# Two feed-forward networks on one core: other weight slots for the second up-chunk and the last down-chunk

## The reference

```
# first block: D_FF = 2816, depthwise conv of width 3 over the tokens
h2 = modulate(rms_norm(x, g_norm2), shift2, scale2)
u = causal_depthwise_conv(h2 @ w_up, w_conv, b_conv)
val, gte = split(u, 2)
x = x + (1 + gate2) * ((val * silu(gte)) @ w_down)
# second block: D_FF_2 = 4096
f = square(relu(x @ w_up + b_up)) @ w_down + b_down
x = layer_norm(ALPHA * x + f, ln3_g, ln3_b)
```

## Time and profile before

| what | value |
|---|---|
| time, median of 3 runs | 3761.49 us (3753.72 to 3762.09) |
| profiled execution, time | 3759.51 us |
| its span | 3757.8 us |
| PE busy | 3127.0 us (83%) |
| DVE, ACT, POOL busy | 1794.4, 955.4, 963.9 us |
| first network, first to last matmul | 933.62 to about 1703.7 us |
| second network, first to last matmul | 2995.02 to about 3715.0 us |

### The profile page before, as it was taken

The page is one execution under the profiler, slowest core; times in us unless marked ns, Lnnn a source line. Parts: engine busy times, 40 slices in busy tenths (PEclk is TensorE's granted clock), DMA queues, the critical chain, the costliest instruction groups (busy, mean ns, idle before and its releaser), DMA issues. The chain is left out here.

```text
span 3757.8 us, 42220 instructions
## 1 busy us (share of the span) xinstructions
PE 3127.0 (83%) x16524; PEld 2674.7 (71%) x16524; DVE 1794.4 (48%) x2896; ACT 955.4 (25%) x1387; POOL 963.9 (26%) x336
## 2 busy tenths in 40 slices
PE   8687999676899999974858637978888699999994
PEld 6576999475688888863746636778668678888883
DVE  1411767335355555456168956872233433333334
ACT  0101544221222122212056534641222211111111
POOL 0312332112223232223012422211301233333333
PEclk9798999587999999986978868999899799999997
DMA  7462232221101111101122322131132111111101
GB/s 265 103 109 83 67 84 51 101 93 48 45 34 56 45 56 45 45 11 51 59 71 76 113 65 69 49 106 34 45 135 103 44 45 45 45 45 66 46 34 56
DMA packets 111989, 257.33 MB, mean 68 GB/s; under 512 B 49761, under 2 KB 71732, under 8 KB 95591
## 3 DMA queue, kind: packets, MB, share of 16 engines
q1 hardware_dynamic: 110439, 252.24, 20.0%
q0 software_dynamic: 1408, 3.15, 1.5%
HBM read 208.33 MB, written 47.03 MB: 68 GB/s over the span
## 5 line engine op out<-in xcount | busy, mean ns | idle before, releaser
L836 PE MATMUL psum<-h_hi,w_hl 128*128 128x512 f32 x2432 | 756.6, 393 | 27.2 <-POOL w_hl L825 23.2
L825 POOL TENSOR_TENSOR w_hl<-w_raw,w_hl 128x2048 fp32r<-128x2048 f32 x65 | 323.5, 4979 | 1012.8 <-ACT w_hl L819 1012.8
L849 PE MATMUL psum<-w_hl,ffn_a_hi 128*128 128x512 f32 x1728 | 540.0, 394 | 30.3 <-issue 30.3
L836 PEld LDWEIGHTS psum<-h_hi,w_hl 128*128 128x128 f32 x2432 | 460.7, 190 | 125.7 <-POOL w_hl L825 24.4
L836 PE MATMUL psum<-h_lo,w_hl 128*128 128x512 f32 x1216 | 476.8, 392 | 0.0
L610 PE MATMUL psum<-w_hl,h_hi 128*128 128x256 f32 (+1 forms) x2048 | 380.9, 289 | 32.0 <-POOL w_hl L571 14.7
L849 PEld LDWEIGHTS psum<-w_hl,ffn_a_hi 128*128 128x128 f32 x1728 | 326.8, 189 | 102.8 <-issue 31.1
L610 PE MATMUL psum<-h_hi,w_hl 128*128 128x512 f32 (+1 forms) x1152 | 349.7, 388 | 53.1 <-POOL w_hl L571 27.3
L610 PEld LDWEIGHTS psum<-w_hl,h_hi 128*128 128x128 f32 x2048 | 329.3, 198 | 34.1 <-issue 18.7
L571 POOL TENSOR_TENSOR w_hl<-w_raw,w_hl 128x2048 fp32r<-128x2048 f32 (+1 forms) x39 | 177.6, 4555 | 680.3 <-ACT w_hl L563 667.2
L849 PE MATMUL psum<-w_hl,ffn_a_lo 128*128 128x512 f32 x864 | 340.1, 394 | 0.0
(11 more groups left out here) (286 smaller groups left out, 5018.3 us busy)
## 6 DMA issues: line engine op xcount, KB each, us to landing
w_raw<-in_w_up SPq DMA_DIRECT2D x38, 1024.0 KB, 4.8
w_raw<-in_w_down SPq DMA_DIRECT2D x27, 1024.0 KB, 4.8
ada_w<-in_w_ada SPq DMA_DIRECT2D x24, 1024.0 KB, 4.7
w_raw<-in_w_in_T SPq DMA_DIRECT2D x12, 1024.0 KB, 6.9
t_y<-mix SPq DMA_DIRECT2D x24, 512.0 KB, 4.8
w_raw<-in_xa_wkv SPq DMA_DIRECT2D x8, 1024.0 KB, 5.7
w_raw<-in_w_in_G SPq DMA_DIRECT2D x8, 648.0 KB, 5.3
p1G<-sb_stage SPq DMA_DIRECT2D x16, 324.0 KB, 3.7
```

Source lines behind the costliest of these rows:

```text
L825: pool.tensor_tensor(self.k.w_lo[s][:, :], self.k.w_raw[s][:, :], self.k.w_hi[s][:, :].bitcast(F), ALU.subtract).then_inc(self.k.wsem["w_r ...
L836: m = pe.matmul(k.bank[b][:, :], w[:, t * CW + f * P:t * CW + (f + 1) * P], h[:, t, half * 512:half * 512 + 512], start=t == 0 and w is k. ...
L849: m = pe.matmul(k.bank[4 + out % 4][:, :], a[:, f, tile * P:(tile + 1) * P], w[:, f * D + half * 512:f * D + half * 512 + 512], start=f == ...
```

## The change

It changes the two networks alone, and computes the same. In both, the second up-chunk is loaded early into slot 1 instead of the first down-chunk. In the first network slot 0 holds up(0), up(2), up(3) and so on to up(21), and at its end the last down-chunk; slot 1 holds up(1) and then down-chunks 0 to 9. In the second network slot 0 holds up(0) and then down-chunks 0 to 14, slot 1 holds up(1) to up(15) and at its end down(15). The activations for the last down-chunk are written to buffers of their own (`last_hi`, `last_lo`). At the end of the first network PE does 5 outputs of down(9) before up(21) and 11 behind it, and DVE's order there is add 0 to 4, convolution of chunk 20, product, gating of the last down-chunk, convolution of chunk 21, add 5 to 8, product of chunk 21, add 9 to 15. The core of the diff:

```
-        ... self.first = k, uses, (w_up[0, :, :], w_down[0, :, :])
+        ... self.first = k, uses, (w_up[0, :, :], w_up[1, :, :])
...
 # ffn_conv, sync
-                wt.load(sp, 0, 1, w_up[1, :, :])
-                wt.load(sp, 1, 0, w_down[0, :, :])
+                wt.load(sp, 1, 0, w_up[1, :, :])
                 def body(j):
-                    g = j + 1
-                    wt.load(sp, 0, 2 * g, w_up[2 * g, :, :])
-                    wt.load(sp, 0, 2 * g + 1, w_up[2 * g + 1, :, :])
-                    wt.load(sp, 1, g, w_down[g, :, :])
+                    wt.load(sp, 0, 2 * j + 1, w_up[2 * j + 2, :, :])
+                    wt.load(sp, 1, j + 1, w_down[j, :, :])
+                    wt.load(sp, 0, 2 * j + 2, w_up[2 * j + 3, :, :])
                 looped(sp, G - 1, body)
+                wt.load(sp, 0, NF1 - 1, w_down[G - 1, :, :])
...
 # ffn_conv, tensor
-                looped(pe, G - 2, body)
-                down(G - 1, range(16))
+                looped(pe, G - 3, body)
+                up(NF1 - 2)
+                down(G - 2, range(5))
+                up(NF1 - 1)
+                down(G - 2, range(5, 16))
+                pe.wait_ge(*wt.at("w_ready", 0, NF1))
+                pe.wait_ge(a_lo_done, NF1)
+                for o in range(16):
+                    down_products(k, pe, last_hi, last_lo, o, dn_mm,
+                                  lambda: pe.wait_ge(dn_out, 16 * (G - 1) + o - 3), 0)
...
 # ffn_conv, scalar, start
-                w_up_hi(0)
-                evac_first(0, 0)
-                w_up_hi(1)
+                wt.split_hi(act, 0, 0)
+                wt.split_hi(act, 1, 0)
+                evac_first(0, 0)
+                w_up_hi(2)
                 silu(0, 0)
                 evac_first(1, 1)
-                w_up_hi(2)
+                act.wait_ge(up_mm, 8)
                 w_down_hi(0)
...
 # ffn_conv, scalar, end
+                a_part(2 * g, 0, last_hi)
                 evac(2 * g + 1, 1)
-                w_down_hi(g)
-                a_part(2 * g, 0)
+                act.wait_ge(up_mm, 4 * NF1)
+                act.wait_ge(w_gated, 2 * G)
+                wt.split_hi(act, 0, NF1 - 1)
                 silu(2 * g + 1, 1)
-                a_part(2 * g + 1, 1)
+                a_part(2 * g + 1, 1, last_hi)
...
 # ffn_conv, vector, end
-                looped(dve, G - 1, body)
+                looped(dve, G - 2, body)
+                add_down(G - 2, range(5))
+                conv_steps(NF1 - 2, 0, False)
+                times_silu(NF1 - 2, 0)
+                gate_w_down(G - 1, 0, NF1 - 1)
+                conv_steps(NF1 - 1, 1, False)
+                add_down(G - 2, range(5, 9))
+                times_silu(NF1 - 1, 1)
+                add_down(G - 2, range(9, 16))
                 add_down(G - 1, range(16))
...
 # ffn_squared_relu, sync
+                wt.load(sp, 0, 0, w_up[0, :, :])
                 def body(g):
-                    wt.load(sp, 0, g, w_up[g, :, :])
-                    wt.load(sp, 1, g, w_down[g, :, :])
-                looped(sp, G, body)
+                    wt.load(sp, 1, g, w_up[g + 1, :, :])
+                    wt.load(sp, 0, g + 1, w_down[g, :, :])
+                looped(sp, G - 1, body)
+                wt.load(sp, 1, G - 1, w_down[G - 1, :, :])
...
 # ffn_squared_relu, scalar
+                act.wait_ge(up_mm, 4 * G)
+                wt.split_hi(act, 1, G - 1)
+                act.wait_ge(squared, G)
+                act.activation(last_hi[:, :, :], r[:, :, :], ACT.Copy).then_inc(a_hi_done, 1)
```

More of the change, by code:

```diff
@@ L785, in __init__ @@
     def __init__(self, k, uses, w_up, w_down):
-        self.k, self.uses, self.first = k, uses, (w_up[0, :, :], w_down[0, :, :])
+        self.k, self.uses, self.first = k, uses, (w_up[0, :, :], w_up[1, :, :])
         self.early_done = {"load": 0, "hi": 0, "lo": 0}
@@ L826, in split_lo, with up_products @@
                                ALU.subtract).then_inc(self.k.wsem["w_ready"][s], 1)
-def up_products(k, pe, hh, hl, mm):
+def up_products(k, pe, hh, hl, mm, slot=0):
+    w_hi, w_lo = k.w_hi[slot], k.w_lo[slot]
     for f in range(2):
@@ L834, in up_products, with down_products @@
             for t in range(KT):
-                for w, h in ((k.w_hi[0], hh), (k.w_lo[0], hh), (k.w_hi[0], hl)):
+                for w, h in ((w_hi, hh), (w_lo, hh), (w_hi, hl)):
                     m = pe.matmul(k.bank[b][:, :], w[:, t * CW + f * P:t * CW + (f + 1) * P],
                                   h[:, t, half * 512:half * 512 + 512],
-                                  start=t == 0 and w is k.w_hi[0] and h is hh,
+                                  start=t == 0 and w is w_hi and h is hh,
                                   stop=t == KT - 1 and h is hl)
             m.then_inc(mm, 1)
-def down_products(k, pe, a_hi, a_lo, out, mm, waits):
+def down_products(k, pe, a_hi, a_lo, out, mm, waits, slot=1):
     tile, half = out // 2, out % 2
@@ L847, in down_products @@
     for f in range(2):
-        for n, (w, a) in enumerate(((k.w_hi[1], a_hi), (k.w_lo[1], a_hi), (k.w_hi[1], a_lo))):
+        for n, (w, a) in enumerate(((k.w_hi[slot], a_hi), (k.w_lo[slot], a_hi), (k.w_hi[slot], a_lo))):
             m = pe.matmul(k.bank[4 + out % 4][:, :], a[:, f, tile * P:(tile + 1) * P],
@@ L869, in ffn_conv @@
         a_lo = k.sb(c, "ffn1_a_lo", [P, 2, S], R)
+        last_hi = k.over("ffn1_last_hi", [P, 2, S], R, raw_at)
+        last_lo = k.sb(c, "ffn1_last_lo", [P, 2, S], R)
         cw = k.sb(c, "ffn1_conv", [P, NF1, 2, 4])
@@ L1003, in _ @@
                 wt.split_lo(pool, 0, 0)
-                looped(pool, G - 1, lambda g: group(g, True))
-                group(G - 1, False)
+                wt.split_lo(pool, 1, 0)
+                wt.split_lo(pool, 0, 1)
+                wt.split_lo(pool, 1, 1)
+                a_part(0, 0)
+                a_part(1, 1)
+                looped(pool, G - 2, group)
+                wt.split_lo(pool, 0, NF1 - 2)
+                a_part(NF1 - 2, 0, last_hi, last_lo)
+                wt.split_lo(pool, 0, NF1 - 1)
+                a_part(NF1 - 1, 1, last_hi, last_lo)
             @block.vector
@@ L1072, in ffn_squared_relu @@
         a_lo = k.sb(c, "ffn2_a_lo", [P, 2, S], R)
+        last_hi = k.sb(c, "ffn2_last_hi", [P, 2, S], R)
+        last_lo = k.sb(c, "ffn2_last_lo", [P, 2, S], R)
         bu = k.sb(c, "ffn2_b_up", [P, 2 * G])
@@ L1113, in _, with group @@
+                pe.wait_ge(a_lo_done, G)
+                for o in range(16):
+                    down_products(k, pe, last_hi, last_lo, o, dn_mm,
+                                  lambda: pe.wait_ge(dn_out, 16 * (G - 1) + o - 3), 1)
             @block.scalar
             def _(act):
[L1115 to L1123, removed]
+                def group(g, first=False):
+                    if first:
+                        wt.split_hi(act, 1, 0)
+                        act.wait_ge(up_mm, 4)
+                    else:
+                        act.wait_ge(up_mm, 4 * g + 4)
+                        wt.split_hi(act, 1, g)
+                        act.wait_ge(dn_mm, 16 * g)
+                    wt.split_hi(act, 0, g + 1)
@@ L1130, in _, with group @@
+                act.activation(last_hi[:, :, :], r[:, :, :], ACT.Copy).then_inc(a_hi_done, 1)
             @block.gpsimd
             def _(pool):
[L1132 to L1134 removed]
+                def group(g):
                     wt.split_lo(pool, 1, g)
+                    wt.split_lo(pool, 0, g + 1)
                     pool.wait_ge(a_hi_done, g + 1)
```

78 lines of the change are left out of this document (44 added, 34 removed).

## The result

The kernel after takes 3713.41 us (median of 4 runs, 3710.77 to 3717.0), beside 3759.97 us (4 runs) for the kernel before: a ratio of 0.988, with a 95% interval of 0.9862 to 0.9897, so 46.6 us or 1.2% faster. The forecast was 3707 us, with 3698 to 3718 as its range. The profiled execution after has a span of 3709.0 us and a time of 3710.77, the lowest of its four.

What follows compares the result with a forecast made beforehand. The number of matmuls on PE bounds the networks' middles, so only PE's 53.5 us of waits and 11.4 us of clock could yield; 19.4 + 13.2 + 8.3 + 12.7 = 53.6 us off gave 3707 us, range 3698 to 3718.

Steps and rivals of the forecast that it cites:

- The four places: Start and end of both networks, where PE waited: gains of 19.4, 13.2, 8.3 and 12.7 us, together 53.6 us.
- Start of the first network: Up(0)'s last bank to up(2)'s end: 44.9 us instead of 64.3, since up(1) is split early; gain 19.4 us.
- The two stops: Before up(1) and up(2) of the first network: PE waits 0.7 us each for the banks' read-out and signalling.
- Down(0) does not wait: First network: a_lo of chunk 1 ready between 998 and 1003, down(0) due at 1002; no wait taken, 1 us kept.
- The middle costs nothing: Loops of the networks: engine order stays, paired 1 MB loads land within 10 us, before they are needed; cost nothing.
- End of the first network: From up(20)'s last bank: 75.4 us against 88.6, despite a new 6.4 us wait before output 9; gain 13.2 us (9 to 19).
- a restart at 2.3: Behind the new wait in down(9): mean clock loss of 2.3 us added, bounds 0 and 3.0.
- Second network: Start 22.6 us instead of 30.9, gain 8.3; down(15) ends at 3702.3 instead of 3715.02 without a wait, gain 12.7.
- The clock's price: Half clock after PE's waits: 1.7 to 3.0 us lost per restart, 2.3 on average; the skill's page gave 0.8.
- The 3713: Whole kernel: alternative time with 0.8 us instead of 2.3 for four restarts fewer, sum about 48 us; no term used it.
- The rival of short stops: Three new stops of 0.7 to 0.85 us bring the clock down, 1.7 to 3.0 us each: 3712 to 3716; chance 4%.
- All later stages shift as they are: Everything behind the four places keeps its length, so the span falls by the full 53.6 us, 3757.8 to 3704.2.

Runs made afterwards that it cites:

- second profile of the kernel before: The kernel before run once more without edit ("before, again"): span 3760.2 us, median 3763.54 us of 12 runs, ratio 1.0003 to the kernel before.
- shared last buffers: Kernel after, but the second network's last activations go into a_hi and a_lo instead of own buffers: 3722.42 us (1 run), second network 710.0 us.
- waits for single banks: Kernel after, but PE waits before each bank of an up-chunk for that bank's read-out alone, not all four: 3705.56 us (1 run).
- the three measurements: Kernel after measured three times without edit, against the kernel before on the same chip: medians 3713.41, 3715.58 and 3711.36 us.
- either half alone: Kernel after with only own last buffers or only the slot 1 move kept in the second network's end: 3722.08 and 3722.42 us (1 run each).

## Why the prediction was right, and where it was off

The median of 3713.41 us lies inside the range of 3698 to 3718, but 1.4 us above the 3703 to 3712 that the forecast gave as its own. The four places and their mechanisms came out as written. What is missing came in elsewhere, and part of it stays open. (The prediction's own sum, 3705.9 + 2.0, is 3707.9; it was put down as 3707.)

- **Start of the first network**, 44.9 us and a gain of 19.4. Measured 955.53 to 1001.18 = 45.65, against 64.3: 18.7. The two stops cost 1.07 us each, not the 0.7 taken.
- **Down(0) does not wait.** Right; the list of waits has no such line. POOL's low part of activation 1 ends at 995.33 + 2.41 = 997.74, 3.4 us before up(2)'s last bank is read, and just ahead of the 998 to 1003 forecast.
- **The middle costs nothing.** Up(2)'s last bank to up(20)'s: 1021.39 to 1615.15 before, 1001.18 to 1594.94 after, 593.76 us both times. The new order of the loads is hidden whole.
- **End of the first network**, 75.4 us with a wait of 6.4 and a restart at 2.3. Measured 1670.06 - 1594.94 = 75.1 us; the wait is 6.34, placed behind output 8 and released by DVE's add, and the convolution took 9.16 us as its row of before (9.10). The restart: 7 outputs at 1.40 and 16 at about 1.39 are 32.0 us, and took 1670.06 - 1636.08 = 34.0, so 2.0. Gain 13.4, forecast 13.2.
- **Second network**: 8.3 and 12.7 forecast, of 720.0. From up(0)'s last bank (2990.27) to up(1)'s (3013.25) 23.0 us instead of 30.9, 8.0 gained; the rest 665.5 to 652.8, 12.7 gained. No wait before down(15).
- **The clock's price.** Behind long waits it was 1.7 to 3.2 us in ten cases, never the 0.8 us worked out from the Trainium skill's section on HAM oscillation ("TensorE: Matmul & The Clock Gate"). The Trainium skill's kernel may restart otherwise; for this one the rows decide. The 3713 that the prediction worked out with that price is close to the median by luck: the four places gained 52.8 us, not 48. The rival of short stops fails for the 0.78 and 0.94 us stops, but has a point for those of 2 us.
- **What failed is the step "All later stages shift as they are"** and the use of one profile's total. The four places gained 52.8 us of the 53.6 forecast. But up(0) itself took 955.53 - 930.60 = 24.9 us instead of 23.4 in the first and 24.6 instead of 23.5 in the second network, and the stretch between the networks 4.3 us more, with 3.0 us less before the first. So the spans differ by 48.8 us. The medians differ by 46.6: for the kernel after the profiled run was the fastest of four. Up(0) is no price of the change: it took 24.7 us in the first network in the second profile of the kernel before and 24.6 in the unchanged second network of the run that changed the first, and 23.5 in the new first network with shared last buffers and with waits for single banks.
- **How sure is the gain?** The medians of before and after differ by 46.6, 44.1 and 52.5 us in the three measurements, the networks by 50 to 53 in every pairing of their profiles. The last of the three fits the networks, the other two fall short of them.
- **Open: does the change cost something between the networks?** In the three kernels whose first network is the old one, this stretch took 1291.3, 1294.5 and 1294.2 us, mean 1293.3; in the eleven with a new one 1293.5 to 1302.1, mean 1296.9. Single profiles of one kernel differ by 6.5 us. Most of that scatter arises in the attention, from DVE's last `top_rank` to its last `dsa_o`: 296.3 and 299.7 us in the two profiles of before, 294.4, 302.3 and 296.4 in the three of after. The means differ mostly behind it, up to the second network: 494.9, 495.1 and 496.9 us with the old first network, 496.3 to 500.2 with a new one, means 495.63 and 498.47. The ranges overlap, and no run changes this part alone. It stays open whether those 2.8 us are scatter or a cost of the change.

## What to carry to other kernels

Where the steady state is bound by one engine, look at its list of waits: each double buffer here had a first and a last use that it did not cover, and all four edges could be costed to about a microsecond from rows of the same trace. At such an edge look for every step that stands in series and free them together: either half alone kept 3 of 12.7 us here. Before moving work off a held operation, look at which operation it will lie beside next.

## What the runs showed of the hardware

- A VectorE operation with two SBUF inputs can stand still until a POOL subtraction ends. Of four steps of 1.27 to 1.28 us one took 5.57 beside a split that ended at 1631.96, so that the four took 9.16 us and not 4.87, and one product of 1.23 us took 4.61 beside another; both ended 1.1 us after the split. The split beside the steps was longer too, 5.29 us against 4.62 beside adds. Adds that read one input from PSUM kept their pace beside a split, at 0.69 us each (at 1617.95).
- The granted clock fell over waits of 2.04 and 2.65 us, but not over one of 2.67, and in the first of these it fell after the matmuls had resumed. The same wait of 7.8 us cost 3.0 us in one profile and 2.1 in another.
- A stop listed as 0.78 us in dense matmuls costs 1.07 us, with the clock at its upper level throughout.
